# Routing of the dense tiles in eight steps that wait for GpSimd's low parts, 25 dots per tile, 25 early rows per gathered tile

## What is computed

```python
q = (ht @ w_q).reshape(PEER_CHUNK, PEER_HEADS, 2, PEER_HALF)
s = jnp.einsum('thpc,hpnc->thpn', q, subkeys)
sv, si = lax.top_k(s, PEER_TOPK)                       # 16 of 128 keys, for each half
cand_s = sv[:, :, 0, :, None] + sv[:, :, 1, None, :]   # 16 x 16 sums
top_s, top_pos = lax.top_k(cand_s, PEER_TOPK)          # 16 experts a head, 128 a token
gate = jax.nn.softmax(top_s, axis=-1)
act = gelu(jnp.einsum('thkd,td->thk', u[expert], ht))
out = jnp.einsum('thk,thkd->td', gate * act, v[expert])
```

## Time and profile before

| | |
|---|---|
| median of 3 runs | 2698.17 us (2696.26 to 2700.51) |
| the profiled execution's own time | 2695.91 us |
| its span, first to last instruction | 2694.1 us |
| TensorE's mean granted clock | 0.988 of 2.4 GHz |

### The profile page before, as it was taken

How to read it: one execution, slowest core, us unless ns; L and a number is a source line. 1 busy time by engine, 2 the same in 40 slices (tenths; PEclk the granted TensorE clock), 3 DMA queues, 4 the chain that set the end, 5 groups by cost and what they waited for, 6 DMA issues and landing times.

```text
span 2694.1 us, 41571 instructions
## 1 busy us (share of the span) xinstructions
PE 2599.7 (96%) x15177; PEld 2331.7 (87%) x15177; DVE 2137.5 (79%) x4586; ACT 883.9 (33%) x1656; POOL 1488.0 (55%) x960
## 2 busy tenths in 40 slices
PE   7999989999999999999999999988999999999998
PEld 6777758999999999999999999976887888788887
DVE  6122273589888999999999996769998898998996
ACT  4223252222222222236666663222222222222222
POOL 1111120245666677776565557847776676676770
PEclk9999989999999999999999999999999999999999
DMA  4110013334877899999999999999999999999993
GB/s 148 47 32 24 24 56 118 110 113 152 294 271 256 306 315 319 325 329 371 382 383 370 377 389 370 404 339 381 389 387 368 386 387 389 357 385 388 381 384 127
DMA packets 296526, 763.33 MB, mean 283 GB/s; under 512 B 25808, under 2 KB 116304, under 8 KB 293584
## 3 DMA queue, kind: packets, MB, share of 16 engines
q0 software_dynamic: 110592, 402.70, 39.9%
q1 hardware_dynamic: 161280, 288.88, 31.2%
q10 hardware_dynamic: 24528, 70.26, 6.8%
HBM read 669.47 MB, written 92.27 MB: 283 GB/s over the span
## 4 chain that ended last, share of the span: by engine, by line
PE 61%; DVE 8%; DMA 8%; issue 6%; POOL 3%; ACT 1%; SPq 0%; DVEq 0%; ACTq 0%; POOLq 0%
PE bank L1650 29%; PE bank L2032 11%; PE wide L2032 8%; DMA g_raw<-g_d 6%; PE bank L2003 5%; PE bank L1899 3%; PE bank L1918 2%; DVE u_row L1384 2%; POOL w_lo L683 1%; DVE v_lo L1601 1%; POOL u_row L699 1%; DVE a_lo L1558 1%; DMA u_row<-in_v,ids 1%; POOL u_row L694 1%; DVE yg L1594 1%
## 5 line engine op out<-in xcount | busy, mean ns | idle before, releaser
L742 POOL DMA_INDIRECT d_row<-in_v,ids x344 | 589.9, 1715 | 279.4 <-DVE yg L1594 196.8
L1650 PE MATMUL bank<-h_hi,w_hi 128*128 128x320 f32 (+1 forms) x2368 | 562.2, 319 | 12.5 <-POOL w_lo L683 11.0
L1650 PE MATMUL bank<-h_hi,w_lo 128*128 128x320 f32 (+1 forms) x2368 | 545.8, 312 | 1.4 <-issue 1.4
L1650 PE MATMUL bank<-h_lo,w_hi 128*128 128x320 f32 (+1 forms) x2368 | 544.7, 311 | 0.0
L683 POOL TENSOR_TENSOR w_lo<-w_raw,w_hi 128x1024 fp32r<-128x1024 f32 x144 | 352.3, 2447 | 283.2 <-ACT w_hi L963 200.5
L1384 DVE CUSTOM_DVE_ANT_0 u_row<-wide,u_row 128x1024 f32<-128x1024 f32 x384 | 449.7, 1222 | 21.3 <-DMA u_row<-in_u_rows,ids 18.6
L694 POOL DMA_INDIRECT u_row<-in_u_rows,ids x384 | 387.8, 1010 | 108.2 <-issue 79.5
L1594 DVE SCALAR_TENSOR_TENSOR yg<-d_row,uh,yg 128x1024 f32<-128x1024 f32 x344 | 426.5, 1279 | 1.4
L1650 PEld LDWEIGHTS bank<-h_hi,w_hi 128*128 128x128 f32 x2368 | 392.5, 189 | 18.2 <-ACT act_st L957 8.7
L1650 PEld LDWEIGHTS bank<-h_lo,w_hi 128*128 128x128 f32 x2368 | 398.7, 188 | 2.5
L1650 PEld LDWEIGHTS bank<-h_hi,w_lo 128*128 128x128 f32 x2368 | 397.3, 188 | 3.6 <-issue 1.1
(11 more groups left out here) (232 smaller groups left out, 4323.8 us busy)
## 6 DMA issues: line engine op xcount, KB each, us to landing
w_raw<-in_u SPq DMA_DIRECT2D x128, 512.0 KB
v_raw<-in_v ACTq DMA_DIRECT2D x126, 512.0 KB
act_d<-act_st SPq DMA_DIRECT2D x128, 320.0 KB
g_d<-g_st SPq DMA_DIRECT2D x20, 2048.0 KB
a_raw<-act_d SPq DMA_DIRECT2D x154, 256.0 KB
g_raw<-g_d SPq DMA_DIRECT2D x120, 256.0 KB
w_raw<-in_w_q SPq DMA_DIRECT2D x32, 512.0 KB
w_raw<-in_w_in SPq DMA_DIRECT2D x20, 512.0 KB
```

What stands on the lines that cost most here:

```text
L742: nc.gpsimd.indirect_dma_start(d_row[k % DR][:, :], None, v_rows, bass.IndirectOffsetOnAxis(ids[:, c:c + 1], 0)).then_inc(d_in[k % DR], 16)
L1650: ins = pe.matmul(banks[h][:, 0:n], lhs[:, part], rhs[:, k, h * n:(h + 1) * n], start=(k == 0 and lhs is lhs_hi and rhs is h_hi), stop=(k ...
```

## The change

`SLOT_DOTS` cuts a dense tile's routing into eight steps. Ahead of step k of tile t, DVE now waits until GpSimd has made the low part of item 45 + 8t + k. The dots of a tile are 25 instead of 22 and stand within the steps as 2, 3, 3, 4, 2, 4, 2, 5. GpSimd may now ask for as many rows by an item as the steps up to then use, and two more. `EARLY` goes from 20 to 25, and one unit of a group has one late row fewer.

From these the other counts follow. 217 rows are asked or used by the end of the routing, which were 202, so 57 are left for the row stage, which were 62: 7 dots and 50 early rows, which were 22 and 40. There are 334 late rows: 15 in group 0, 22 in each of groups 1 to 6, 21 in each of groups 7 to 14, and 19 in group 15.

```diff
-ROWS_TILE = 22
+SLOT_DOTS = (2, 3, 3, 4, 2, 4, 2, 5)
+SLOTS = len(SLOT_DOTS)
+ROUTE_ITEM = 45
+ROWS_TILE = sum(SLOT_DOTS)
...
-EARLY = 20
+EARLY = 25
...
-ROWS_UNIT = (2, 2, 2, 2, 2, 3, 2, 2, 3, 2)
+ROWS_UNIT = (2, 2, 2, 2, 2, 3, 2, 2, 2, 2)
...
+def dots_before(m):
+    t, k = divmod(min(m, DT * SLOTS), SLOTS)
+    return ROWS_Q + ROWS_TILE * t + sum(SLOT_DOTS[:k])
...
-                return ROWS_Q + (ROWS_FRONT - ROWS_Q) * (t - 2 * BODY1) // (2 * B0 - 2 * BODY1)
+                return dots_before(max(t - ROUTE_ITEM, 0)) + (2 if t >= ROUTE_ITEM else 0)
...
+            def slot(t, k):
+                if t < DT:
+                    dve.wait_ge(lo_done, W_U0 + ROUTE_ITEM + SLOTS * t + k + 1)
+
+            def slot_dots(t, k):
+                for r in range(SLOT_DOTS[k] if t < DT else 0):
+                    dot_row()
...
+                slot(t, 0)
                 group([sums(0, CUT1, 0, 1, TOP), sums(CUT1, CUT2, 1, 4, 8), sums(CUT2, CUT3, 4, 8, 4),
...
-                for r in range(rows):
-                    dot_row()
+                slot_dots(t, 0)
...
+                slot(t, 1)
                 V.tensor_tensor(route[:, 2, t, :].rearrange("p (h k) -> p h k", h=PH), top2[:, :, :],
...
+                slot(t, 2)
...
-                    for r in range(rows if half else 0):
-                        dot_row()
+                    slot_dots(t, 2 + 2 * half)
+                    slot(t, 3 + 2 * half)
                     group([V.tensor_tensor(eq[:, :, :, :], place[:, half, :, :].unsqueeze(3).broadcast_to(shape),
...
+                    slot_dots(t, 3 + 2 * half)
+                    slot(t, 4 + 2 * half)
                     group([V.tensor_tensor(eq[:, :, :, :], eq[:, :, :, :],
...
+                if t + 1 < DT:
+                    slot_dots(t, 6)
+                    slot(t, 7)
+                    slot_dots(t, 7)
```

More of the change, by code:

```diff
@@ L1407, in gate_rows, with best_pairs @@
                                 ALU.mult).then_inc(uh_gate, 1)
-            def best_pairs(t, rows=0):
+            def slot(t, k):
[4 more added lines that the diff above has]
+                    dot_row()
+            def best_pairs(t):
                 one, two = top1[:, t, :, 0, :], top1[:, t, :, 1, :]
@@ L1431, in best_pairs, with pair_keys @@
                       + [V.max_index(pos[:, 0, h, 8:16], top2[:, h, 8:16], rest_c[:, h, :]) for h in range(PH)])
-            def pair_keys(t, rows=0):
+                slot_dots(t, 1)
+            def pair_keys(t):
+                slot(t, 2)
                 group([V.tensor_scalar(pos[:, 1 + k, :, :], pos[:, 0, :, :], bits, None, ALU.bitwise_and)
@@ L1476, in _ @@
             for t in range(DT):
[L1477 to L1482, removed]
+                best_pairs(t)
+                pair_keys(t)
+                if t + 1 < DT:
+                    slot_dots(t, 6)
+                    slot(t, 7)
+                    slot_dots(t, 7)
             dve.wait_ge(g_e, 1)
```

## The result

The changed kernel takes 2740.91 us (median of 6 runs, 2735.30 to 2745.60), the kernel before 2697.43 (6 runs, 2696.26 to 2700.51). The ratio is 1.0165, 95% interval 1.0153 to 1.0177: slower by 1.65%, where 2681 us was forecast and 2692 was the top of the range. The span of the profiled execution is 2740.7 us, 46.6 more than before.

The account below looks back on a forecast made before the run. TensorE, busy 96% of the span, was taken as the bound, with DMA limiting the last stage's first half. Terms +1.3 - 1 - 2.5 - 15 = -17.2 from 2695.9 gave 2678.7, as a median 2681 us; range 2663 to 2692.

Parts of the forecast that it names:

- The last stage: Groups 1 to 14: fewer late rows a group keep the DMA queue from falling back; -15 us, between -12.2 and -18.9.
- all transfer waits go: Rival for the last stage: earlier late rows also clear the hole at 1847 us; -34 us, 2664 us, chance 0.13.
- latency, not rate: Rival for the last stage: transfer waits are of latency, so one row fewer changes little; about -3, 2695 us, chance 0.14.
- Start of the last stage: Late rows asked 6 to 9 us earlier stop competing with first v chunks; TensorE's 2.60 us hole goes: -2.5 (0 to -4).
- Row stage: GpSimd has 5 asks fewer but more early rows, net 2.7 us less work at the end; -1 us (-3 to +3).
- Gate stage: Rows per pair of strips unchanged, ask and use shift together: 0 us.
- Routing stage: DVE keeps up at 53.6 us a tile; slightly late low parts cost little: +1.3 us (-0.7 to +4.3).
- signs of being wrong: Holes staying with 21 rows, new holes in group 15, or TensorE waiting for low parts in every eighth item.
- The slower rival: Routing stage: collisions stay, DVE bounds it at 59.6 us a tile, TensorE stalls 25 us; +9, 2707 us, chance 0.07.
- The steps do nothing: Rival for the routing stage: DVE always behind its steps, no wait holds, only counts work; time within the main case.
- my sum: Whole kernel: +1.3 - 1 - 2.5 - 15 = -17.2 us against the profiled 2695.9.

Follow-up runs that it names:

- The seven kernels with the new counts, no lock and no mending: Changed kernel with ROUTE_ITEM 46 (with or without waits), even asks, 0 or 3 rows beyond; kernel before with new counts, even or stepped asks: 0.9969 to 0.9977.
- the kernel with only the counts: Kernel before with 25 dots a tile, 25 early rows and the new ROWS_UNIT, asks and order of work as before: 2693.74 us, ratio 0.9973.

## Why the prediction was wrong

*The last stage: right.* -15 was forecast for groups 1 to 14, -14.5 came. The 15 was picked between bounds of 12.2 and 18.9, so that it is this close is in part luck; that the later holes go is not. The holes at 2040 and 2300 have no successor. The hole in group 1 stayed, with a second one behind it. Timeline of PE, changed kernel:

```profile
1906.70 1.22 PE L2055 MATMUL wide<-v_hi,a_hi 128*128 128x512 f32 x2 [6.77 <-DVE y L1601]
...
1932.66 0.79 PE L2055 MATMUL wide<-v_hi,a_hi 128*128 128x512 f32 x1 [5.10 <-DVE y L1591]
```

So "all transfer waits go" is refuted, and so is "latency, not rate": one or two rows fewer a group did clear the later holes. DVE's waits on `g_raw` fell from 40.1 us to 23.5 (waits view, DVE, 1836 to 2735 us):

```profile
DVE prod L1567 <- DMA g_raw<-g_d: 23.5, 7, 9.0
```

*Start of the last stage: right.* -2.5 forecast, -2.9 in group 0; the hole of 2.60 us is gone. *Row stage:* -1 forecast, +0.7, inside its bounds but with the other sign. *Gate stage:* 0 forecast, 0.5.

*Routing stage: wrong, and the whole miss.* +1.3 (-0.7 to +4.3) was forecast, 59.7 came. The step that failed is this sentence: "The steps start these operations right behind the low part, which should take them away: 53.6 us, so DVE keeps up and waits some 3 us a tile." It takes for granted that DVE arrives at a step ahead of the low part. It arrived a step behind, so no wait ever held it. One of the signs of being wrong came with it: TensorE waited 24 times for low parts. The estimate of its free speed was fair: 53.6 us for a tile, 52.0 by the sum above. What I didn't work out is what starts the *next* low part: GpSimd's asks wait for dots, and the change puts these a fixed distance behind. That fixed when each low part starts, at the very moment when DVE starts an operation that a low part holds up. I costed "two to four such collisions" a tile from the earlier trace rows as chance events; by the change they became six a tile, each at its full price.

*The slower rival* had the right sign and cause (the collisions stay, asks wait for `row_used`, low parts wait behind them, TensorE stalls), but chance 0.07 and a price of 59.6 us a tile with 25 us for the stage. The tile took 67.3. It counted the collisions of before, and 5 us a tile of stall; it lacked the feedback, in which each lengthened operation delays the ask that sets the next low part. *"The steps do nothing"* was put within the main case. Its premise was true (no wait ever held), its conclusion was not: the asks are part of the steps, and with the dots they do a great deal.

*Even without the lock* my sum was too good. The seven kernels with the new counts, no lock and no mending come to 0.9969 to 0.9977, -6 to -8 us and not -17. In the kernel with only the counts the last stage up to group 15 gives 18.5 us (816.2 for 834.7), but items 45 to 86 take 6.4 us more than before and the gate stage 4.2 (430.1 us for 425.9). I had +1.3 and 0 for these.

*What stays open.* That the tie and the coincidence make the lock is shown by the runs that change one number. Why DVE enters the stage a step behind in the change and not with the asks an item later was not isolated. Nor did I try to keep the asks at 2 and shift only DVE's start.

## What to carry to other kernels

When operations of two engines can hold each other up, an ask of one that waits for the newest work of the other can set a phase between them. Collisions are then not an average: in the change they came at six of eight low parts in tile after tile, with one row more at none of the comparisons. Before costing such a step, write down for each engine what releases its next colliding instruction, to the microsecond, and try the distance at a few values; here one row less or more was worth some 30 and 52 us by the ratios. A wait that is meant to order two engines does nothing if the waiting one is already late: look at who arrives first, and by how much.

## What the hardware showed

A comparison (128x2048, bf16) of 2.29 us took 4.79 beside a GpSimd subtraction of 2.37 us whose record begins 0.27 us behind its own, and 3.60 when it began 1 us behind the subtraction: in both it ended 2.15 to 2.17 us behind the subtraction's end. So the record that begins first is not always that of the operation that runs first. Begun 0.56 us ahead of an ask, the comparison kept its 2.29 us and the ask took 2.54 instead of 0.94. That the small operations suffer as much was new to me: a subtraction of 128x128 (L1447) that takes 0.29 us alone took 2.92. The dots kept their 1.22 us beside low parts (the one at 1060.76 of the change, beside the low part of 1060.31); one of their two inputs, `wide`, lies in PSUM.
